# Low parts of up-projection weight tiles from an adding transfer instead of VectorE differences

## The reference

```
def sq_relu_mlp(h, w_up, w_down):
    return jnp.square(jax.nn.relu(h @ w_up)) @ w_down
...
        h = rms_norm(x, ln_mlp_pre[i])
        f = sq_relu_mlp(h, mlp_w_up[i], mlp_w_down[i])
        x = x + rms_norm(f, ln_mlp_post[i]).astype(x.dtype)
```

## Time and profile before

| | |
|---|---|
| median of 3 runs | 1897.83 us |
| profiled execution | 1897.43 us, span 1895.6 us |
| TensorE busy | 1888.5 us, 9432 matmuls |
| VectorE busy | 1344.0 us |
| ScalarE busy | 987.4 us |
| VectorE, low parts (L2109, WR to WL) | 330 of 1.22 us |
| ScalarE, high parts (L1346, WR to WH) | 331 of 1.06 us |
| GpSimd, adding transfers in WR (in_quart) | 48 of 512 KB, 6.4 us to landing |

### The profile page before, as it was taken

One profiled execution on the slowest core, in us unless ns is written; L12 is line 12 of the kernel. 1 busy time (PEld: TensorE's weight loads), 2 busy tenths in 40 slices (PEclk: granted clock), 3 DMA queues, 4 the chain that ended last, 5 costly groups with the idle time before them and its releaser, 6 DMA issues. The chain is left out here.

```text
span 1895.6 us, 25342 instructions
## 1 busy us (share of the span) xinstructions
PE 1888.5 (100%) x9432; PEld 1554.5 (82%) x9432; DVE 1344.0 (71%) x2000; ACT 987.4 (52%) x1591; POOL 96.1 (5%) x114
## 2 busy tenths in 40 slices
PE   9999999999999999999999999999999999999999
PEld 8877888888888788888888988667788888888887
DVE  8656665556566766665666788998897877767867
ACT  5634464454546756454544335788435455545454
POOL 0100000101000000000100000000000000100101
PEclk9999999999999999999999999999999999999999
DMA  7632156758323124766742346232234634654735
GB/s 232 157 100 100 66 152 174 168 161 216 119 67 143 45 67 131 192 147 176 178 154 68 122 134 170 87 94 73 90 96 138 167 89 156 157 149 116 199 96 122
DMA packets 70684, 249.79 MB, mean 132 GB/s; under 512 B 7970, under 2 KB 8226, under 8 KB 69924
## 3 DMA queue, kind: packets, MB, share of 16 engines
q1 hardware_dynamic: 56448, 198.82, 31.2%
q0 software_dynamic: 13824, 49.29, 15.1%
q10 hardware_dynamic: 292, 0.07, 0.0%
HBM read 246.05 MB, written 2.10 MB: 131 GB/s over the span
## 5 line engine op out<-in xcount | busy, mean ns | idle before, releaser
L553 PE MATMUL ps<-HH,WH 128*128 128x512 f32 (+1 forms) x1676 | 623.4, 372 | 0.0
L555 PE MATMUL ps<-HH,WL 128*128 128x512 f32 (+1 forms) x1676 | 618.4, 369 | 0.0
L554 PE MATMUL ps<-HL,WH 128*128 128x512 f32 (+1 forms) x1676 | 618.2, 369 | 0.0
L1346 ACT ACTIVATE WH<-WR 128x1024 fp32r<-128x1024 f32 x331 | 346.9, 1056 | 473.3 <-PE ps L555 308.9
L2109 DVE TENSOR_TENSOR WL<-WR,WH 128x1024 fp32r<-128x1024 f32 x330 | 400.7, 1219 | 260.0 <-ACT WH L1346 259.3
L553 PEld LDWEIGHTS ps<-HH,WH 128*128 128x128 f32 x1676 | 316.2, 189 | 62.3 <-issue 10.0
L555 PEld LDWEIGHTS ps<-HH,WL 128*128 128x128 f32 x1676 | 316.2, 189 | 53.0
L554 PEld LDWEIGHTS ps<-HL,WH 128*128 128x128 f32 x1676 | 316.3, 189 | 51.2
L1006 PE MATMUL ps<-WL,AH 128*128 128x512 f32 x490 | 190.9, 390 | 0.0
L1005 PE MATMUL ps<-WH,AL 128*128 128x512 f32 x490 | 190.8, 389 | 0.0
L1004 PE MATMUL ps<-WH,AH 128*128 128x512 f32 x490 | 190.8, 389 | 0.0
(11 more groups left out here) (401 smaller groups left out, 2616.0 us busy)
## 6 DMA issues: line engine op xcount, KB each, us to landing
WR<-in_up SPq DMA_DIRECT2D x96, 512.0 KB, 4.4
WR<-in_quart SPq DMA_DIRECT2D x60, 512.0 KB, 3.5
WR<-in_quart POOLq DMA_DIRECT2D x48, 512.0 KB, 6.4
WR<-in_in SPq DMA_DIRECT2D x48, 512.0 KB, 3.5
WR<-in_down SPq DMA_DIRECT2D x16, 512.0 KB, 3.5
WR<-in_quartf SPq DMA_DIRECT2D x14, 512.0 KB, 3.5
WR<-in_quartf POOLq DMA_DIRECT2D x14, 512.0 KB, 5.7
MT<-in_up SPq DMA_DIRECT2D x12, 512.0 KB, 3.8
```

Source lines behind the costliest of these rows:

```text
L553: e.matmul(ps, wh, hi[:, c, cols], start=c == 0 and not (shared and h), stop=False, skip_group_check=shared)
L554: e.matmul(ps, wh, lo[:, c, cols], start=False, stop=False, skip_group_check=shared)
L555: y = e.matmul(ps, wl, hi[:, c, cols], start=False, stop=c == x.n - 1, skip_group_check=shared)
L1346: e.activation(x.wh[:, 0:n], raw(m, x.raw)[:, 0:n], AF.Copy).then_inc(*k.mark("whi", u))
```

## The change

For 28 of the 32 up units of each layer (the last four of group 0 and all of groups 1, 2 and 3) VectorE no longer makes the low part. ScalarE writes the rounded high part to WH as before, and with a second activation minus the same rounded value to WL. GpSimd then issues a transfer that reads the weight tile from memory a second time and adds it into WL, which leaves the weight minus its high part. TensorE waits for this landing. The transfers use two semaphores by turns ("lower0", "lower1"), and each waits for the one before last. The raw buffer of such a unit is free when ScalarE's second activation is done. The two semaphores of the token blocks are replaced by two that are otherwise used later in the program.

```
+            units.append(Unit(t, size, wh, wl, event, r, prior, twice=j >= twice(tiles)))
...
-            add(f"up{layer}{o}", up[8 * o:8 * o + 8])
+            add(f"up{layer}{o}", up[8 * o:8 * o + 8], twice=lambda tiles: 0 if o else 4)
...
-        add(f"up{layer}3", up[24:])
+        add(f"up{layer}3", up[24:], twice=lambda tiles: 0)
...
-            e.wait_ge(*k.on("wlo", u))
+            e.wait_ge(*k.on(f"lower{u % 2}" if x.twice else "wlo", u))
...
+    if x.twice:
+        e.activation(x.wl[:, 0:n], raw(m, x.raw)[:, 0:n], AF.Copy, scale=-1.0).then_inc(*k.mark("whi", u))
...
-    a_mean(e, k, "pre", "mix0", 2, m.X[:, 2, :], ("x_in2",))
+    a_mean(e, k, "pre", "mix0", 2, m.X[:, 2, :], ("distance0", "tokens"))
...
-        if u not in k.ahead:
+        if u not in k.ahead and not k.units[u].twice:
...
+def g_lower(e, k, name):
+
+    u = k.at[name]
+    for j in range(u, u + 8):
+        x = k.units[j]
+        if x.twice:
+            e.wait_ge(*k.on("whi", j))
+            if k.count.get(f"lower{j % 2}"):
+                e.wait_ge(*k.on(f"lower{j % 2}", "last"))
+            e.dma_start(x.wl[:, 0:128 * x.n], x.ap.bitcast(F32R), accum_op=A.add).then_inc(*k.mark(f"lower{j % 2}", j, by=16))
+            k.also(f"lower{j % 2}", "last")
...
         for o in range(3):
+            g_lower(e, k, f"up{layer}{o}")
             g_seven(e, k, layer, o)
+        g_lower(e, k, f"up{layer}3")
...
-        e.wait_ge(*k.on("wlo", x.prior))
+        e.wait_ge(*k.on("whi" if k.units[x.prior].twice else "wlo", x.prior))
```

More of the change, by code:

```diff
@@ L89, with __init__ @@
 class Unit:
-    def __init__(self, ap, n, wh, wl, freed, raw, prior, more=None, sum_of=None):
+    def __init__(self, ap, n, wh, wl, freed, raw, prior, more=None, sum_of=None, twice=False):
         self.ap, self.n, self.wh, self.wl, self.freed = ap, n, wh, wl, freed
-        self.raw, self.prior, self.more, self.sum_of = raw, prior, more, sum_of
+        self.raw, self.prior, self.more, self.sum_of, self.twice = raw, prior, more, sum_of, twice
 class Dry:
@@ L173, in split_slot, with add @@
         return m.WH[:, s, :], m.WL[:, s, :], event
-    def add(name, tiles, n=DC, extra=None, freed=None):
+    def add(name, tiles, n=DC, extra=None, freed=None, twice=len):
         at[name] = len(units)
@@ L185, in add @@
             raw_user[r] = len(units)
-            units.append(Unit(t, size, wh, wl, event, r, prior))
+            units.append(Unit(t, size, wh, wl, event, r, prior, twice=j >= twice(tiles)))
     def seven(name, quarters, slots={}, extra={}):
@@ L1540, in a_gla @@
             a_cut(e, k, u + 2)
-    a_mean(e, k, "pre", "mix0", 2, m.X[:, 2, :], ("x_in2",))
+    a_mean(e, k, "pre", "mix0", 2, m.X[:, 2, :], ("distance0", "tokens"))
     a_cut(e, k, u + 3)
-    a_mean(e, k, "pre", "mix0", 3, m.X[:, 3, :], ("x_in3",))
+    a_mean(e, k, "pre", "mix0", 3, m.X[:, 3, :], ("distance1", "tokens"))
     a_split(e, k, "mix0", 2)
@@ L3233, in sync_program @@
     fetch(e, k, 2)
-    e.dma_start(m.X[:, 2, :], d["x"][2]).then_inc(*k.mark("x_in2", by=16))
+    e.dma_start(m.X[:, 2, :], d["x"][2]).then_inc(*k.mark("distance0", "tokens", by=16))
     fetch(e, k, 3)
-    e.dma_start(m.X[:, 3, :], d["x"][3]).then_inc(*k.mark("x_in3", by=16))
+    e.dma_start(m.X[:, 3, :], d["x"][3]).then_inc(*k.mark("distance1", "tokens", by=16))
     e.dma_start(m.WGU[:, :], d["wgu"]).then_inc(*k.mark("par", "wgu", by=16))
```

## The result

The changed kernel takes 1946.73 us in the median of 4 runs, against 1897.80 us for the kernel before; the ratio is 1.0258, 95% interval 1.0246 to 1.0270. Slower was forecast, at 1915 (range 1900 to 1933): the time lies outside, and the loss of 49 us is nearly three times the 17.7 us of the sum.

A forecast was written before the change was run, and what follows sets the result against it. TensorE, busy 1888.5 of 1895.6 us, was taken to bound the kernel. Six late landings (6 × 6.4 − 21.93 = 16.5 us) plus 1.2 us of restarts gave +17.7 us on 1897.4: 1915 us, range 1900 to 1933.

The forecast's parts named there:

- Whatever VectorE is spared here cannot shorten this: In the up and down products TensorE is busy for 300.00 us of 300, so VectorE's 68 us less gains nothing.
- the six changes: Changes from the seven-product stage to an up group; only the first up tile there was to be late, 16.5 us in all.
- 21.93: Summed lead in us at six changes, from the first up tile's adding transfer issue to TensorE's first up matmul; mean 3.66.
- I take 6.4: Landing of an adding transfer at each change, in us: median over 48 of the same size and queue.
- the lone 5.5: Landing in us of an adding transfer by itself; as lower bound it gave 11.1 us of waits at the six changes.
- 7.8: Landing in us of adding transfers in a bunch; as upper bound it gave 24.9 us of waits at the six changes.
- the clock as a rival: Rival: TensorE's clock falls at each stall, half rate costing 3 us per wait, 18 in all, 1933 us; chance 8%.
- the fifth tile: First changed tile of a layer's first up group: 7.39 us for the landing, enough at 6.4, costed at nothing.
- The restart: TensorE's restart after each wait at a change of stage: 0.2 us taken, 1.2 us for six.
- Adding into tiles of the other type: Point for the rival that landings are in time, like a plain load's 3.4 us: 1898.3 us, not slower; chance 8%.
- The chain did not begin earlier: Rival: seven-stage adding transfers land sooner, so the chain starts earlier and each wait is 0.84 us; 1903.7 us; chance 7%.
- The engines did not fill up: Rival: adding transfers take 3.9 us each, so a cycle needs 91 us of 81.6; 55 us more, 1953 us; chance 7%.

The follow-up runs named there:

- none late: Against the changed kernel, the first two up tiles of groups 1 to 3 and first five of group 0 keep VectorE's difference (42 tiles changed): 1897.72 us, ratio 1.0000.
- the loads held back: Against the changed kernel, SyncE's raw load behind a changed tile waits for that tile's adding transfer to land, not ScalarE's second activation: ratio 1.0169, some 1930 us.
- minus first: Against the changed kernel, ScalarE writes minus the high part before the high part, so the adding transfer is issued 0.95 us sooner: 1931.55 us, ratio 1.0180.

## Why the prediction was wrong

**Right: the bound.** "Whatever VectorE is spared here cannot shorten this" is shown by the run with none late: 49 us less of VectorE, and no time gained.

**Right: the place and the lead.** Six waits at the six changes. From the issues to the starts that TensorE would have made (0.227 us behind the last seven matmul) the leads are 2.0, 4.1, 3.0, 4.5, 3.9 and 4.9 us, 22.3 in all; 21.93 was worked out. That the sums agree so well is in part luck: the single leads are off by 0.1 to 1.8 us, both ways (3.82 and 2.68 were worked out for the first two).

**Wrong: the size of the landing.** The term "I take 6.4" is the step that failed: the six landings sum to 57.2 us, not 38.4, which is 18.8 of the 29.4 us that the sum lacks. The prediction saw that "plain loads for the next up tiles are in flight at just this place" and gave them 0.9 us, 6.4 less the lone 5.5; they cost 2.9, the 9.5 with them less the 6.6 without. The 6.4 is a median over transfers that had few loads beside them. From the issues and landings in the traces, a third of a plain load was in flight in the median beside those 48, and 1.1 at the most; beside the six first up tiles it was 2.6 to 4.5, and 0.3 to 0.6 with the loads held back (a load's share of the adding transfer's time to landing, the table of gains counted as two). Nor was 7.8 an upper bound: 12 of the 48 took 8.7 to 12.9 us, each the third or fourth issued in a bunch. That SyncE's loads "wait for ScalarE's second activation instead of VectorE's difference, which is no later" was written down as harmless. It means that the load and the adding transfer have one releaser, and the load, issued 0.27 us sooner, is in front.

**Wrong: the clock as a rival.** It was given 8% as another way that things might go. It is no other way but a consequence of the forecast itself: a wait of 2 us or more was predicted at six places, and each of the six that came is followed by half rate, 10.9 us in all (18 was the estimate). Terms that come with the forecast belong in the sum.

**Wrong: the fifth tile.** Costed at nothing with 7.39 us of lead; in layer 0 its landing took 8.4 us, and 1.05 us of wait is left. The same cause: with the loads held back it lands in 6.7 us, and TensorE doesn't wait. In layer 1 it landed in 6.3 us, in time.

**Right or nearly: the rest.** The restart costs 0.05 us a wait (35.1 us of waits, 57.2 − 22.3 = 34.9 of lateness), less than the 0.2 taken. Adding into tiles of the other type costs the engines no more: the software queue of the changed kernel over 240 to 540 us holds 52 adding transfers (7488 packets, 144 each; 24 are those of the seven stages, as before), 2.9 us each of 16 engines, 3.0 before:

```profile
q0 software_dynamic: 7488, 27.27, 50.0%
q1 hardware_dynamic: 8907, 32.95, 31.9%
```

The chain did not begin earlier on the whole: four leads are longer and two shorter than worked out, 0.4 us in the sum, and at all six changes ScalarE's row still begins behind a landing of the seven stage's own (2.0 to 2.8 us idle). The engines did not fill up over the cycle, which was that rival's condition; they were full for the few microseconds at the change of stage, with a share near 1.00.

## What to carry to other kernels

A time to landing is a property of the moment, not of the transfer: before taking a median, ask what else the same event releases, and on which queue it stands in front. When a product waits at the change from a short stage to a long one, reckon its lead in the short stage's units, and leave the first tiles out. Where TensorE is to wait a few microseconds, add the half rate behind the wait to its price at once, some 2 us for each wait here.

## What was not expected of the hardware

Waits of TensorE as short as 2.0 us bring its granted clock to 0.50: of 25 waits of 2.0 to 8.5 us in these profiles 24 did (one of 2.4 us, with minus first, did not), and none of those of 1.5 us and below. The half rate goes by the wait more than by its length: 1.5 to 3.0 us behind each, 10.9 us for six waits of 35.1 us in the changed kernel and 13.6 us for six of 19.8 us with the loads held back. Useless matmuls in place of the idle time were a net gain of 11 us over the change.
